# Heads of block 1: products and lanes share five PSUM banks, the plan's costs by form of step, decay matrices on GpSimd

## What is computed

```
h = rms_norm(x, norm_pre)
(aq, ak, av, az, dq, dk, dv, db, da, dz, gate_att, gate_dn) = split_cols(h @ w_in)
y_att = (attention(rope(norm(aq)), rope(norm(ak)), av) * silu(az)) @ w_br_att      # 8 heads of 128
q, k, v = silu(short_conv([dq, dk, dv])); q, k = l2_norm(q), l2_norm(k)
g = cumsum(-exp(a_log) * softplus(da + dt_bias)) in a chunk; beta = sigmoid(db)    # two directions, 8 heads
decay = exp(where(tril, g_i - g_j, -inf))
T = inverse(1 + tril(k_beta @ k.T * decay, -1));  a_intra = (q @ k.T) * decay
scan over the chunks: v_new = T @ (v_beta - k_beta * exp(g) @ state); o = q * exp(g) @ state + a_intra @ v_new; ...
y_dn = (rms_norm(o_f + o_b) * silu(dz)) @ w_br_dn
x = x + rms_norm((sigmoid(gate_att) * y_att + sigmoid(gate_dn) * y_dn) @ w_out);  then a gated projection of p
```

## Time and profile before

| | us |
|---|---|
| median of 3 runs | 2147.75 (2145.37 to 2148.02) |
| the profiled execution | 2149.83 |
| its span in the profile | 2148.0 |
| TensorE busy | 2104.3 |
| DVE, ACT, POOL busy | 1275.4, 1054.6, 235.0 |
| mean granted clock of TensorE | 0.997 |

### The profile page before, as it was taken

The page is one execution under the profiler, slowest core; times in us unless marked ns, Lnnn a source line. Parts: engine busy times, 40 slices in busy tenths (PEclk is TensorE's granted clock), DMA queues, the critical chain, the costliest instruction groups (busy, mean ns, idle before and its releaser), DMA issues.

```text
span 2148.0 us, 36022 instructions
## 1 busy us (share of the span) xinstructions
PE 2104.3 (98%) x15046; PEld 1680.9 (78%) x15046; DVE 1275.4 (59%) x2281; ACT 1054.6 (49%) x2046; POOL 235.0 (11%) x240
## 2 busy tenths in 40 slices
PE   7999999999999999999999999999999999999999
PEld 6777777787778887877777888888777777888887
DVE  6777677776755455655567443444577775443442
ACT  6656766676655236656665332323455554222331
POOL 1013222231210011100001000000100101000000
PEclk9999999999999999999999999999999999999999
DMA  4321212222224332111111332222221212232222
GB/s 179 108 75 62 77 68 85 68 77 65 71 80 147 127 137 95 60 59 59 59 59 64 101 114 81 98 98 98 84 64 64 64 59 99 98 103 94 98 100 77
DMA packets 36227, 186.76 MB, mean 87 GB/s; under 512 B 4560, under 2 KB 4944, under 8 KB 16992
## 3 DMA queue, kind: packets, MB, share of 16 engines
q1 hardware_dynamic: 36064, 184.45, 25.1%
HBM read 172.86 MB, written 7.90 MB: 84 GB/s over the span
## 4 chain that ended last, share of the span: by engine, by line
PE 89%; DVE 6%; ACT 3%; issue 1%; DMA 0%; SPq 0%; POOL 0%; DVEq 0%; ACTq 0%
PE ps L1879 87%; ACT arena L2841 1%; PE ps L1882 1%; DVE spl L2337 1%; ACT spl L2844 1%; ACT hh L2841 0%; DVE x L2706 0%; DMA raw<-wstream 0%; DVE x L2464 0%; DVE arena L2356 0%; DVE arena L2649 0%; DVE x L2635 0%; DVE arena L2631 0%; DVE hl L2657 0%; DVE hl L2639 0%
## 5 line engine op out<-in xcount | busy, mean ns | idle before, releaser
L1879 PE MATMUL ps<-hh,spl 128*128 128x512 f32 (+1 forms) x3152 | 1018.2, 396 | 10.9 <-ACT x L2844 2.1
L1879 PEld LDWEIGHTS ps<-hh,spl 128*128 128x128 f32 x3152 | 584.7, 189 | 144.7 <-issue 19.1
L1879 PE MATMUL ps<-hl,spl 128*128 128x512 f32 (+1 forms) x1568 | 616.0, 393 | 0.0
L2337 DVE TENSOR_TENSOR spl<-raw,spl 128x512 fp32r<-128x512 f32 x596 | 427.2, 740 | 159.1 <-ACT spl L2844 158.0
L1879 PE MATMUL ps<-arena_r,spl 128*128 128x512 f32 x1968 | 468.7, 393 | 10.4 <-DVE arena_r L2349 8.5
L1879 PEld LDWEIGHTS ps<-arena_r,spl 128*128 128x128 f32 x1968 | 371.9, 189 | 90.1 <-issue 10.9
L2844 ACT ACTIVATE spl<-raw 128x512 fp32r<-128x512 f32 x596 | 345.1, 619 | 144.4 <-PE ps L1879 138.2
L1879 PEld LDWEIGHTS ps<-hl,spl 128*128 128x128 f32 x1568 | 295.5, 188 | 60.6 <-issue 4.8
L2841 ACT ACTIVATE arena<-arena 128x512 f32<-128x512 f32 (+3 forms) x220 | 142.2, 648 | 187.3 <-DVE arena L2711 141.1
L1879 PE MATMUL ps<-arena 32*32 32x32 f32 (+5 forms) x5664 | 216.9, 224 | 7.5 <-issue 6.1
L1879 PEld LDWEIGHTS ps<-arena 32*32 32x32 f32 (+4 forms) x5664 | 126.1, 115 | 82.3 <-issue 70.6
(11 more groups left out here) (271 smaller groups left out, 2143.1 us busy)
## 6 DMA issues: line engine op xcount, KB each, us to landing
raw<-wstream SPq DMA_DIRECT2D x148, 1024.0 KB, 4.9
arena<-spill SPq DMA_DIRECT2D x17, 256.0 KB, 4.5
GS<-g_rows SPq DMA_DIRECT2D x16, 256.0 KB, 3.3
spill<-x SPq DMA_DIRECT2D x14, 256.0 KB, 2.6
arena<-arena SPq DMA_DIRECT2D x18, 128.0 KB, 2.0
x<-xT SPq DMA_DIRECT2D x4, 512.0 KB, 6.2
spill<-arena SPq DMA_DIRECT2D x8, 256.0 KB, 2.1
x<-xT SPq DMA_DIRECT2D x1, 2048.0 KB, 8.3
```

The costliest lines, as they stand in the source:

```text
L1879: return pe.matmul(out, lhsT, rhs, start=start, stop=stop, skip_group_check=True)
L2337: tt(spl[:, p % 2, 1, c], raw[:, p % 2, c], spl[:, p % 2, 0, c].bitcast(F32), ALU.subtract) \
```

## The change

- `Share` wraps a pool of banks and a greatest number that one user may hold. After the gates' product, banks 0 to 4 form one pool; `main` and `ring` are shares of it of at most three each. After the products with w_br_att `main` becomes banks 0, 1 and 3, and returns to 0 and 1 at the last gate product and after the first q and k of block 2.
- The plan's costs on TensorE are new, and `CHANGE` is a table by the form before and after (wide, narrow, tiled).
- `pr_g` moves from DVE to POOL, as the addition of `off_u` or `off_l` (0 or -1e30) to the whole 128 x 512 of `GS`. The column's g is negated once (`gate_t`) and enters as the bias of the exponential, which is now four instructions on ACT for each matrix. The triangle multiply goes. The copy to `eglast` moves into `pr_q`, and the state's update waits for `pr_qe`.

Cut to its core (other costs are changed in the same manner, for block 2's attention steps too):

```diff
@@ -44,14 +44,17 @@
 NVEC = _at
 
 
-PE_B, DV_B, AC_B, PO_B = 0.86, 0.69, 0.62, 1.25
-PE_S2 = 0.46
+PE_B, DV_B, AC_B, PO_B = 0.866, 0.69, 0.62, 1.25
+PE_S2 = 0.47
 PE_S, DV_S, AC_S, PO_S = 0.21, 0.34, 0.3, 0.6
 MUL, MUL_H = 0.228, 0.117
-PE_H, DV_H, AC_H = 0.44, 0.41, 0.37
+PE_H, DV_H, AC_H = 0.35, 0.41, 0.37
 HOP = 0.08
-CHANGE = 0.088
-ONE_PASS = ("mul", "tok", "ar_ss", "cv_r", "on_b", "st_w", "st_t")
+WIDE, NARROW, TILED = 0, 1, 2
+CHANGE = {(WIDE, TILED): 0.1, (NARROW, TILED): 0.1, (TILED, WIDE): 0.1, (TILED, NARROW): 0.05, (NARROW, WIDE): 0.06}
+FORM = {**dict.fromkeys(("at_o", "at_t", "sc_r", "sc_v", "sc_oq", "sc_s", "sc_o", "tr_k", "tr_v", "pr_kk", "df_t", "df_o"),
+                        NARROW),
+        **dict.fromkeys(("lv_m", "lv_x", "lv_p1", "lv_p2", "lv_q1", "lv_q2", "st_z", "st_o", "df_s"), TILED)}
 TAIL_32 = 0.4
 MARGIN = 0.0
 SLACK = 1.0
@@ -118,6 +121,26 @@
         self.free_at[u.slot] = self.order.bank_free[u.b] = self.order.now
 
 
+class Share:
+
+
+    def __init__(self, pool, most):
+        self.pool, self.most, self.ids, self.out = pool, most, pool.ids, 0
+
+    def ready(self, n=1):
+        return self.out + n <= self.most and self.pool.ready(n)
+
+    def take(self):
+        self.out += 1
+        u = self.pool.take()
+        u.home = self
+        return u
+
+    def give(self, u):
+        self.out -= 1
+        self.pool.give(u)
+
+
 class Operand:
 
 
@@ -159,9 +182,10 @@
         t = max(self.now, after)
         if u:
             st.u, t = u, max(t, u.t)
-        if cost and cost[0][0] == "PE" and self.aside != (kind not in ONE_PASS):
-            self.aside = not self.aside
-            self.clock["PE"] += CHANGE
+        if cost and cost[0][0] == "PE":
+            form = FORM.get(kind, WIDE)
+            self.clock["PE"] += CHANGE.get((self.form, form), 0.0)
+            self.form = form
         for q, c in cost:
             t = self.clock[q] = max(self.clock[q], t + (HOP if cost[0][0] != "PE" or t > self.now else 0.0)) + c
             if q == "PE" and kind[:3] == "lv_":
@@ -520,6 +544,8 @@
     o.main("gate_mm", cost=[("PE", 5.6), ("DV", 0.7)], u=u)
     ring.give(u)
     obank_att, scan_bank = Banks(o, [side[3]]), Banks(o, [side[4]])
+    pool = Banks(o, [0, 1] + side[0:3])
+    main, ring = Share(pool, 3), Share(pool, 3)
 
 
     def decay_lane():
@@ -703,16 +729,16 @@
             while ("g_ld", hd, d) not in o.at or (hd and ("pr_q", hd - 1, d) not in o.at):
                 yield
             o.behind(o.at["g_ld", hd, d], o.at["pr_q", hd - 1, d] if hd else None)
-            yield "DV"
+            yield "AC"
             o.add("pr_a", hd, d, cost=[("AC", AC_B)])
-            yield "DV"
-            o.add("pr_g", hd, d, cost=[("DV", 4 * DV_S)]).ib = decays[hd]
+            yield
+            o.add("pr_g", hd, d, cost=[("PO", 1.4)]).ib = decays[hd]
             if hd < 7:
                 t = o.now
                 o.add("g_ld", hd + 1, d, cost=[("DMA", 4.0)])
                 o.now = t
-            yield
-            o.add("pr_e", hd, d, cost=[("AC", AC_B), ("PO", PO_B)]).ib = decays[hd]
+            yield "AC"
+            o.add("pr_e", hd, d, cost=[("AC", 4 * 0.36)]).ib = decays[hd]
 
     def prep_lane(hd):
 
@@ -740,7 +766,7 @@
         o.behind(o.at["pr_e", hd, 1])
         while not ring.ready(2):
             yield "PE"
-        st = add("pr_kk", hd, cost=[("PE", 1.7), ("DV", 2 * DV_B), ("DV", 8 * DV_S)], hold=True)
+        st = add("pr_kk", hd, cost=[("PE", 1.82), ("DV", 2 * DV_B), ("DV", 8 * DV_S)], hold=True)
         st.u2 = ring.take()
         ring.give(st.u)
         ring.give(st.u2)
@@ -988,6 +1014,7 @@
     for m in range(KT):
         gemm(ya, KT, ya_done(m))
     o.drain()
+    main = Banks(o, [0, 1, side[1]])
     o.main("load_p")
     pa = Operand("p_lo", "p_h", "p_l")
     for m in range(KT):
@@ -1162,6 +1189,7 @@
         o.spawn(f"tail{j}", tail_lane(j, half, u))
 
     o.spawn("r2", r2_lane())
+    main = Banks(o, [0, 1])
     gemm_half(h, lambda j, k: 8 * j + k, 1, z_half, (main, Banks(o, [side[2], side[4]])))
 
 
@@ -1283,7 +1311,7 @@
             isp, old = sp.take()
             o.behind(old)
             yield "PE"
-            st = o.add("st_z", m, kb, cost=[("PE", 0.2 + 0.86 * f)], u=u)
+            st = o.add("st_z", m, kb, cost=[("PE", 0.25 + 0.96 * f)], u=u)
             st.u, st.iqk, st.isp, st.old = u, qk_of[m], isp, old
             yield "AC"
             o.add("st_e", m, kb, cost=[("AC", 0.2 + 0.84 * f)] * 3)
@@ -2434,6 +2463,7 @@
                 elif kind == "gate_t":
                     full(q.u)
                     dve.tensor_copy(GS[0:16, 0, :], psum[q.u.b][0:16, :]).then_inc(drained[q.u.b], 1)
+                    ts(gcol, gcol, -1.0, None, ALU.mult).then_inc(sem("gate_neg"), 1)
 
                 elif kind == "at_s":
                     i = (q.n - 1) % 16
@@ -2482,16 +2512,6 @@
                             w.wait_ge(sem("sc_o"), 4 * old.hd + 4)
                     stt(out=dst, in0=acc_of[q.ia], scalar=scale, in1=pad_of[q.ip], op0=ALU.mult, op1=ALU.mult) \
                         .then_inc(sem("cv_n"), 1)
-                elif kind == "pr_g":
-                    hd, d = q.key
-                    col = d * 8 + hd
-                    w.wait_ge(sem(f"g_ld{d}"), 16 * (hd + 1))
-                    if q.n == 1:
-                        w.wait_ge(sem("gate_col"), 1)
-                    for c in range(4):
-                        i = ts(g4(B_of[q.ib][d])[:, c, :], g4(GS[:, d, :])[:, c, :], g3(gcol)[:, c, col:col + 1], 0.0,
-                               ALU.subtract, ALU.min)
-                    i.then_inc(sem("pr_d"), 1)
                 elif kind == "pr_kk":
                     hd, K = q.hd, keep_of[q.keep]
                     if hd == 0:
@@ -2564,7 +2584,7 @@
                     if s == 0:
                         i = dve.tensor_copy(st[:, :, 1, :], o[:, 0:256].rearrange("p (d n) -> p d n", d=2))
                     else:
-                        w.wait_ge(sem("pr_ld"), at["pr_e", hd, 1].n)
+                        w.wait_ge(sem("pr_qe"), at["pr_q", hd, 1].n)
                         for d in range(2):
                             e0 = (d * 8 + hd) * 4 + chunk(d, s)
                             i = stt(out=st[:, d, (s + 1) % 2, :], in0=st[:, d, s % 2, :],
@@ -3031,7 +3051,12 @@
                 elif kind == "pr_e":
                     hd, d = q.key
                     w.wait_ge(sem("pr_d"), at["pr_g", hd, d].n)
-                    f(B_of[q.ib][d], B_of[q.ib][d], ACT.Exp).then_inc(sem("pr_ed"), 1)
+                    if q.n == 1:
+                        w.wait_ge(sem("gate_neg"), 1)
+                    for c in range(4):
+                        b_, col = g4(B_of[q.ib][d])[:, c, :], d * 8 + hd
+                        i = f(b_, b_, ACT.Exp, bias=g3(gcol)[:, c, col:col + 1])
+                    i.then_inc(sem("pr_ld"), 1)
                 elif kind == "pr_b":
                     empty(q.u)
                     for r in Q32:
@@ -3269,20 +3294,24 @@
                     done, t_ = at["ar_dma", q.key[0]].done, tmp_of.get(q.key[0], ar_tmp)[0]
                     w.wait_ge(sem(done[0]), done[1])
                     tt(t_, t_, cosA, ALU.mult).then_inc(sem("ar_cos"), 1)
-                elif kind == "pr_e":
+                elif kind == "pr_g":
                     hd, d = q.key
-                    e0, D = (d * 8 + hd) * 4, B_of[q.ib][d]
-                    w.wait_ge(sem("pr_eg"), at["pr_a", hd, d].n)
-                    po.tensor_copy(eglast[:, e0:e0 + 4], g4(G_of[d])[:, :, 127 if d == 0 else 0])
-                    w.wait_ge(sem("pr_ed"), q.n)
-                    tt(g4(D), g4(D), bc4(C["tri_u" if d == 0 else "tri_l"]), ALU.mult).then_inc(sem("pr_ld"), 1)
+                    w.wait_ge(sem(f"g_ld{d}"), 16 * (hd + 1))
+                    if hd > 1:
+                        w.wait_ge(sem("pr_b"), hd - 1)
+                        t = at["lv_q2", hd - 2].u
+                        w.wait_ge(drained[t.b], t.n)
+                    tt(g4(B_of[q.ib][d]), g4(GS[:, d, :]), bc4(C["off_u" if d == 0 else "off_l"]), ALU.add) \
+                        .then_inc(sem("pr_d"), 1)
                 elif kind == "pr_q":
                     hd, d = q.key
+                    e0, LG = (d * 8 + hd) * 4, G_of[d]
                     w.wait_ge(sem("pr_eg"), at["pr_a", hd, d].n)
                     if q.k_old:
                         w.wait_ge(sem("sc_o"), 4 * q.k_old.hd + 4)
                     w.wait_ge(sem("cv_n"), at["cv_n", hd].n)
-                    tt(keep_of[q.keep][f"qe{d}"], q_tile[hd % 2], G_of[d], ALU.mult).then_inc(sem("pr_qe"), 1)
+                    po.tensor_copy(eglast[:, e0:e0 + 4], g4(LG)[:, :, 127 if d == 0 else 0])
+                    tt(keep_of[q.keep][f"qe{d}"], q_tile[hd % 2], LG, ALU.mult).then_inc(sem("pr_qe"), 1)
                 elif kind == "lv_0":
                     w.wait_ge(sem("pr_b"), q.n)
                     tt(dc32(hC0), dc32(hB), level_mask(0), ALU.mult)
@@ -3347,7 +3376,8 @@
```

(8 more changed lines are left out.)

25 lines of the change are left out of this document (12 added, 13 removed).

## The result

| | before | after |
|---|---|---|
| median of 8 runs | 2147.89 us | 2154.86 us (2151.47 to 2156.85) |
| the profiled execution, its span | 2149.83, 2148.0 | 2155.93, 2154.1 |

A forecast was written before the change was run, and what follows sets the result against it. TensorE, busy 2104.3 of 2148.0 us, was taken as the bound. Terms -5.5 + 1 - 1.5 - 0.5 = -6.5, rounded to -6.0: 2149.83 - 6.0 - 2.08 = 2141.75 us, range 2135.5 to 2150.5.

The forecast's parts named there:

- Product banks: In block 1's heads, a third bank removes TensorE's waits for product banks: 5.5 us recovered, bounds 4.2 and 8.
- x, pad and silu rows: In the heads, five TensorE stops for ACT's copies and DVE's silu that free product banks: 3.2 us, to be recovered.
- What the lanes lose: Lanes left with two banks instead of three may deliver results late: +1 us, bounds -5.4 and +5.4.
- Issue stops: Seven TensorE stops in the heads where nothing the profile shows was missing: 7.8 us, expected to stay near that.
- The plan's costs: New costs bring the plan's TensorE clock nearer the chip's: -1.5 us in the heads, 0 elsewhere, bounds -4 and +4.
- Decay: In the heads, decay matrices' subtraction moves to GpSimd, DVE -14.0 us, ACT +9.8: net -0.5 us, bounds -2 and +3.
- the rival built on ACT held by GpSimd: In the heads, ACT waiting for GpSimd's addition holds bank copies behind it: about +5 net, 2153 us, chance 0.15.
- The sum: All terms together: -6.5 us, rounded to -6.0, taken from the profiled execution and corrected to the median: 2141.75 us.
- I am wrong if: Failure signs: TensorE's named waits in the heads stay above 6 us, or block 2's attention moves more than the heads.

The follow-up runs named there:

- e8: e4 with the products' share of the five pooled banks cut from three to two; 2150.59 us.
- e4: The changed kernel with the old charge for changes of form (0.088 us) from block 2's second layer on; 2145.17 us.
- e7: The changed kernel with the slack for placing lane steps 2.0 us instead of 1.0 in block 2's second layer; 2141.93 us.
- e5: The kernel before with only the new table of form changes, and that only from block 2's second layer on; 2169.41 us.
- e17: The kernel before with one plan cost, DV_B (a DVE operation on a whole bank), 0.70 instead of 0.69; 2151.42 us.
- e2: The kernel before with only the decay matrices' subtraction moved to GpSimd and the exponential in four parts; 2147.01 us.
- e12: e7 with the slack of 2.0 us also from head 6 on, to the end of the plan; 2134.75 us.
- e10: The changed kernel without its decay part, with the old charge for changes of form from block 2's second layer on; 2187.71 us.
- e11: The changed kernel without shared banks and third bank, with the old charge for changes of form from block 2's second layer on; 2162.11 us.
- e16: e12 with one plan cost, DV_B (a DVE operation on a whole bank), 0.70 instead of 0.69; 2143.98 us.

## Why the prediction was wrong

- *Product banks, -5.5 (4.2 to 8).* The mechanism held inside the heads: the 3.2 us of x, pad and silu rows are gone. But e8 shows that this can't be put down to the number of banks alone.
- *What the lanes lose, +1 (-5.4 to +5.4).* In the heads the lane waits went from 4.4 to 5.5 us, +1.1. I read only the stretch in which lanes run, though. Another 2.6 us came behind it, at the split of the w_br_att weights (`DVE arena_r` 1.9 and `ACT arena` 0.6, from 650 to 806), where before had no idle time that could have warned me. Issue stops fell from 7.8 to 5.4 for no reason found: after, e4 and e7 have one list up to block 2's second layer, and in these three executions A stood at -1.9, -1.0 and -4.8. The heads as a whole gave 1 to 5 us of the 6.
- *The plan's costs, -1.5 us in the heads and 0 elsewhere (-4 to +4 together).* This is the step that failed. From A to C the changed kernel lost 8.0 us against before and 9.3 against e4, which differs from it only from block 2's second layer on. The table alone makes such a loss (e5), through the place of the last head's last steps (e7, which has the table and not the place, and e17, which has the place and not the table). I had read the idle time of block 2's first attention (5.4 us) and written that it was too small to gain much and could double, and then set the term to 0; the second attention I hadn't read, and there the idle time went from 4.8 to 13.0. The sum had no term for the clock behind stops either (up to 3.6 us here), though the earlier trace rows showed one; against before that isn't part of the miss, since before loses as much elsewhere. The mistake beneath it: small idle time was taken for a small stake. What bounds the loss is the chain that lies hidden under the last products (11.0 us, 2.05 to spare), which is in the trace of before.
- *Decay, -0.5.* e2 gives -1.1 us against before beside it, which can't be told from none. ACT +11.0 in the heads as expected (9.8). DVE -19.2 for -14.0: its 120 splits of weights took 737 ns in the mean, for 786. GpSimd's additions took 1539 ns, where I had counted the multiplies' 1345. As foreseen they waited for a load of g (once, 21.7 us) and not for ACT, and no wait of ACT for GpSimd is seen in the heads. So the rival built on ACT held by GpSimd isn't what made it slower; its number, 2153, was near by accident.
- *The sum.* Without the last attention's loss (e4, 2145.2) the time lies in the range, 3.4 us above the forecast. What "I am wrong if" named, block 2's attention moving by more than the heads, is what happened. But that is luck in part: the sum was made of parts that the runs show not to be additive, and it holds for this one list. A small slip in it changes nothing: the text counts five bank stops first and six after; the rows have six.

That the two kernels differ by 7 us says little about the change: 0.01 us in one cost moves before by 2.4, after by 7.4 and e12 by 9.2. What stays open: which property of a list makes the heads lose up to 38 us (in e10 and e11 the loss is many stops of up to 7.5 us, for lanes as well as for banks, and the lower clock behind them), and whether e12 is a better rule or a better draw; e16, 9 us above it, speaks for the latter. The time that the plan's own TensorE clock has reached at its end goes with the measured times (correlation 0.85 over the twenty kernels, lowest for e12 and highest for e10), with a scatter of 6 us about the line.

## What to carry to other kernels

Where a planner sets the order from costs, a change of its costs or resources draws a new order: price it by the spread that a meaningless nudge gives (here 2 to 9 us), not by the idle time that it aims at, and measure the nudge before the parts. At every point where products need the last results of lanes, measure in the trace how long the hidden chain is and how much it has to spare; that is the stake, even if the stretch shows no idle time. A marker in the trace compares two orders only if the same work lies ahead of it: count the matmuls. A lead of the products over the lanes inside a stage is worth only what is left of it behind the stage.

## What the runs showed of the hardware

A stop of TensorE can cost more than its length, but doesn't always. In the stretches of 20 us with stops of 2.4 and 3.6 us the granted clock was 0.91, up to 1.8 us more each; in e5, with stops in a row, 0.79, up to 4.2 us more. But the same stop for ACT at the start of block 2's second attention (1.8 us) came with a clock of 0.91 in before and 1.00 in after, and in after a stop of 2.5 us that ended at 868 came with 1.00. Before, and then after:

```profile
1520.00:1540.00 20.00, 18.17 (x68) 13.26 (x67) 10.58 (x27) 10.43 (x19) 1.80 (x1) 0.91 0.26 91
...
1529.21 1.51 PE L1879 MATMUL ps<-arena,cst 128*128 128x512 f32 x2 [1.83 <-ACT arena L2841]
```

```profile
1520.00:1540.00 20.00, 17.53 (x70) 12.67 (x69) 12.88 (x21) 9.12 (x15) 3.09 (x2) 1.00 0.20 61
...
1524.39 1.12 PE L1908 MATMUL ps<-arena,cst 128*128 128x512 f32 x2 [1.82 <-ACT arena L2861]
...
860.00:880.00 20.00, 16.94 (x112) 15.37 (x112) 12.95 (x30) 13.84 (x36) 3.71 (x5) 1.00 0.15 53
```

What decides it no run here shows. Also, the same list of instructions gave A 3.8 us apart in two executions (e4 and e7), with 5.9 and 4.3 us of issue stops from 60 to 660 us, and 3.7 us apart in before and e5. A difference of under 4 us in one stage of one profile can't be read as an effect.
